# Splitting the remaining input projections into rounded pairs and reordering the first attention of a hybrid decoder block

## What is computed

```python
mod = silu(c) @ w_ada + b_ada            # 6 vectors of 1024: shift/scale/gate for mixer (a) and ffn (f)
h = rms_norm(x, g_attn) * (1 + sc_a) + sh_a
proj = h @ w_in                          # 1024 x 3072, cut into dq, dk, dv, sq, sk, sv (512 each)
# A: differential attention, 4 heads, two 64-wide q/k maps, 128-wide values, QK norm, ALiBi
a = softmax(q0 k0 + bias) - lam * softmax(q1 k1 + bias);  a_out = rms_norm(a @ dv) * 0.8
# B: stick-breaking attention, 8 heads of 64, strictly causal
a = exp(log_sigmoid(z) + suffix_sum(log_sigmoid(-z)));    b_out = rms_norm(a @ sv)
x = x + gt_a * (concat(a_out, b_out) @ w_out)
h = rms_norm(x, g_ffn) * (1 + sc_f) + sh_f
x = x + gt_f * hier_moe(h)               # top-1 of 4 groups, then top-2 of 8 SwiGLU experts of 256
```

## Time and profile before

| what | value |
|---|---|
| median of 3 runs | 682.06 us (679.41 to 684.06) |
| the profiled execution's own time | 682.16 us |
| its span | 680.0 us |
| PE busy | 561.3 us, 83% of the span, 2832 matmuls |
| DVE busy | 275.7 us, 41% |
| ACT busy | 170.2 us, 25% |
| chain that ended last | PE 67%, DMA 14%, SPq 7%, DVE 7%, ACT 3% |

### The profile page before, as it was taken

The page is one execution under the profiler, slowest core; times in us unless marked ns, Lnnn a source line. Parts: engine busy times, 40 slices in busy tenths (PEclk is TensorE's granted clock), DMA queues, the critical chain, the costliest instruction groups (busy, mean ns, idle before and its releaser), DMA issues.

```text
span 680.0 us, 7324 instructions
## 1 busy us (share of the span) xinstructions
PE 561.3 (83%) x2832; PEld 330.4 (49%) x2832; DVE 275.7 (41%) x474; ACT 170.2 (25%) x310; POOL 82.2 (12%) x98
## 2 busy tenths in 40 slices
PE   3379989999989899999999925988998898788740
PEld 2347768446455445665445613544554454344410
DVE  3866680553734455655012275222322232222005
ACT  7045541221222336786133210000000000000002
POOL 8331100000000000000021202111121112010000
PEclk9999999997998899999999955999999999889985
DMA  8984753537120007000751382899999999999719
GB/s 344 407 271 168 276 211 134 185 124 247 62 92 33 1 0 308 2 0 1 293 232 62 129 335 70 319 417 416 416 416 417 415 417 417 418 417 417 315 42 355
DMA packets 42384, 163.24 MB, mean 240 GB/s; under 512 B 7796, under 2 KB 7796, under 8 KB 34164
## 3 DMA queue, kind: packets, MB, share of 16 engines
q1 hardware_dynamic: 31972, 134.52, 49.6%
q0 software_dynamic: 9248, 26.23, 10.9%
q10 hardware_dynamic: 1136, 2.11, 0.8%
HBM read 158.64 MB, written 12.58 MB: 252 GB/s over the span
## 4 chain that ended last, share of the span: by engine, by line
PE 67%; DMA 14%; SPq 7%; DVE 7%; ACT 3%; issue 2%; POOLq 0%; DVEq 0%; ACTq 0%
PE banks L1582 11%; PE banks L1280 10%; PE banks L1474 8%; PE banks L1333 8%; PE banks L1601 6%; PE banks L1285 4%; DMA stage<-in_w_in_dram 4%; DMA stage<-in_w_dram 4%; DMA qkT<-in_w_dram 4%; PE banks L1426 3%; PE banks L1410 2%; PE banks L1570 2%; DMA stage<-pair_rows 2%; SPq L371 2%; PE banks L1355 1%
## 5 line engine op out<-in xcount | busy, mean ns | idle before, releaser
L1601 PE MATMUL banks<-stage,work 128*64 128x512 f32 x168 | 63.1, 638 | 10.0 <-ACT work L767 5.8
L1280 PE MATMUL banks<-hT,stage 128*128 128x512 f32 x144 | 66.4, 616 | 1.5 <-DMA stage<-in_w_in_dram 1.5
L1582 PE MATMUL banks<-qkT,work 128*64 128x256 f32 x272 | 63.6, 391 | 0.0
L765 ACT ACTIVATE work<-banks 128x256 f32<-128x256 f32 x16 | 6.1, 384 | 222.6 <-PE banks L1582 222.6
L1474 PE MATMUL banks<-stage,mixT 128*128 128x512 f32 x128 | 56.2, 594 | 0.0
L1185 DVE TENSOR_TENSOR work<-banks,gates 128x1024 f32<-128x1024 f32 x16 | 19.6, 1225 | 85.5 <-PE banks L1601 85.5
L1582 PE MATMUL banks<-hT,work 128*64 128x256 f32 x192 | 45.2, 394 | 2.6 <-DMA qkT<-in_w_dram 2.6
L799 DVE SCALAR_TENSOR_TENSOR mixT<-stage,small,mixT 128x1024 f32<-128x1024 f32 x35 | 44.9, 1282 | 3.5 <-DMA stage<-in_w_ada_dram 2.8
L1280 PEld LDWEIGHTS banks<-hT,stage 128*128 128x128 f32 x144 | 27.9, 199 | 34.0 <-issue 31.5
L1180 DVE TENSOR_TENSOR work<-work,banks 128x256 f32<-128x256 f32 x16 | 6.7, 421 | 88.3 <-ACT work L765 88.3
L534 POOL DMA_INDIRECT pair_rows<-work,tables x16 | 16.1, 1005 | 202.4 <-DVE work L1185 202.4
(11 more groups left out here) (263 smaller groups left out, 1089.4 us busy)
## 6 DMA issues: line engine op xcount, KB each, us to landing
stage<-in_w_dram SPq DMA_DIRECT2D x31, 1024.0 KB, 20.5
qkT<-in_w_dram SPq DMA_DIRECT2D x23, 1024.0 KB, 20.9
stage<-in_w_ada_dram POOLq DMA_DIRECT2D x16, 1024.0 KB, 5.6
stage<-in_w_in_dram SPq DMA_DIRECT2D x6, 2048.0 KB, 10.1
hT<-in_w_dram SPq DMA_DIRECT2D x12, 1024.0 KB, 18.2
val<-in_w_dram SPq DMA_DIRECT2D x10, 1024.0 KB, 18.4
mixT<-in_w_dram SPq DMA_DIRECT2D x10, 1024.0 KB, 18.6
alibi<-in_w_dram SPq DMA_DIRECT2D x5, 1024.0 KB, 23.6
```

The costliest lines, as they stand in the source:

```text
L1280: ins = mm(bank, w[:, k, ch * P:(ch + 1) * P], hT[:, k, :], start=(k == 0), stop=(k == KD - 1))
L1582: ins = mm(banks[half * C:(half + 1) * C, 2, up * F:(up + 1) * F], heT[:, r, k * P + half * C:k * P + (half + 1) * C], ws[2 * place + half ...
L1601: ins = mm(banks[half * C:(half + 1) * C, 4 + 2 * r + col, :], geT[:, fc * P + half * C:fc * P + (half + 1) * C], w2s[2 * place + half][:, ...
```

## The change

- **Jobs.** All 24 projection jobs run split now (`project`). Chunk 0 is rounded and subtracted by POOL; chunk 12 is rounded by ACT behind the last head evacuation, into a spare 128x1024 place (as chunk 16 later); chunks 13 to 23 are rounded in attention steps 0 to 8 (`split_at`), on ACT behind `exp_unit(s)` and on DVE behind `max_unit(s)` and the quarter.
- **Head order.** The two gate jobs stand ahead of the four v jobs.
- **Steps.** A step's jobs stand directly behind `scores(s)` on PE, ahead of `probT_make(s-1)`. Step 8 has no projection, step 15 has two halves; the column sum, the router product and the two late gate jobs move to steps 8, 12 and 14. The late adaLN quarters are summed in steps 0, 2, 4, 6, 8, 9, 10, 11.
- **Loads.** POOL's first adaLN quarter waits for the first piece of `w_in`; each gate bias row load stands behind its vector's quarters.
- **Memory.** `hT_hi` lies over x, `hT_lo` over `hT` itself; x is loaded again (2 MB) after the last v job, and POOL's additions wait for it. DVE does its four `hT_lo` subtractions after all eight `hT_hi` copies.

```diff
-    head = [("qk", n) for n in range(8)] + [("v", t, 0) for t in range(NT)] + [("gate", 0, 0), ("gate", 0, 1)]
+    head = [("qk", n) for n in range(8)] + [("gate", 0, 0), ("gate", 0, 1)] + [("v", t, 0) for t in range(NT)]
-        for _ in range(2 if s < 8 else 1):
+        for _ in range({8: 0, 15: 2}.get(s, 2 if s < 8 else 1)):
-    steps[7].append((("col", 3), None))
-    steps[9] += [(("gate", 1, 0), None), (("shift_router",), None)]
-    steps[11].append((("gate", 1, 1), None))
+    steps[8] += [(("col", 3), None), (("shift_router",), None)]
+    steps[12].append((("gate", 1, 0), None))
+    steps[14].append((("gate", 1, 1), None))
+ADA_STEPS = (0, 2, 4, 6, 8, 9, 10, 11)
...
+        hT_hi = rounded("hT_hi", [P, KD, T], "xr")
+        hT_lo = rounded("hT_lo", [P, KD, T], "hT")
+        w_hi_spare = rounded("w_hi_spare", [P, KD, P], "work", 3072)
...
+        def split_at(s):
+            return {0: (13,), 6: (19, 20), 7: (21, 22), 8: (23,)}.get(s, (s + 13,) if s < 6 else ())
+        def hi_before(n):
+            return {12: None, 16: 12, 20: 8}.get(n, n - 4 if n >= 4 else None)
```

SP, behind the loads of `w_in` and `w_out`:

```diff
             sp.wait_ge(job_done, job_no[("v", 3, 1)] + 1)
+            sp.dma_start(xr[:], x_rows).then_inc(x_again, 16)
```

POOL:

```diff
-            for n, v in enumerate((GATE_A, GATE_F)):
-                g.dma_start(gates[:, n, :], row(b_ada[:, v * D:(v + 1) * D])).then_inc(gate_bias_in, 16)
+            raw, hi, lo, arrived, value = split_chunk(0)
+            pool.wait_ge(arrived, value)
+            g.tensor_copy(hi, raw).then_inc(w0_hi, 1)
+            pool.wait_ge(w0_hi, 1)
+            g.tensor_tensor(lo, raw, hi.bitcast(F32), ALU.subtract).then_inc(w0_split, 1)
...
                     if n == 0:
                         pool.wait_ge(scale_used, KD // 2)
+                        pool.wait_ge(piece_in[0], 16)
...
+                for u, vec in enumerate((GATE_A, GATE_F)):
+                    if v == vec:
+                        g.dma_start(gates[:, u, :], row(b_ada[:, v * D:(v + 1) * D])).then_inc(gate_bias_in, 16)
+            pool.wait_ge(x_again, 16)
```

ACT:

```diff
-                if n >= 4:
-                    act.wait_ge(job_done, n - 3)
+                if hi_before(n) is not None:
+                    act.wait_ge(job_done, job_no[chunk_job(hi_before(n))] + 1)
+                if n == 12:
+                    act.wait_ge(norm_done, 8)
...
             for job in head_jobs:
                 job_evac(job)
+            w_round(12)
...
                 if s < NT * DH:
                     exp_unit(s)
+                for n in split_at(s):
+                    w_round(n)
```

DVE:

```diff
             for job in head_jobs:
                 job_evac(job)
+            w_rest(12)
...
-                if s < 8:
-                    ada_quarter(SCALE_F + s // 4, s % 4)
+                if s in ADA_STEPS:
+                    i = ADA_STEPS.index(s)
+                    ada_quarter(SCALE_F + i // 4, i % 4)
+                for n in split_at(s):
+                    w_rest(n)
```

PE:

```diff
+            def project(job, bank, ks):
...
+                if c == 0:
+                    pe.wait_ge(w0_split, 1)
+                    for k in ks:
+                        pe.wait_ge(hT_hi_ready, k + 1)
+                        mm(bank, w_hi[:, k, part], hT_hi[:, k, :], start=(k == 0), stop=False)
+                        mm(bank, lo[:, k, part], hT_hi[:, k, :], start=False, stop=False)
+                    pe.wait_ge(hT_lo_dve, KD // 2)
+                    pe.wait_ge(hT_lo_pool, KD // 2)
+                    for k in ks:
+                        ins = mm(bank, w_hi[:, k, part], hT_lo[:, k, :], start=False, stop=(k == KD - 1))
+                    return ins
+                pe.wait_ge(w_split, c)
+                hi = chunk_hi(c)
+                for k in ks:
+                    mm(bank, hi[:, k, :], hT_hi[:, k, :], start=(k == 0), stop=False)
+                    mm(bank, hi[:, k, :], hT_lo[:, k, :], start=False, stop=False)
+                    ins = mm(bank, lo[:, k, part], hT_hi[:, k, :], start=False, stop=(k == KD - 1))
...
                 if s < NT * DH:
                     scores(s)
+                for job, part in step_parts.get(s, ()):
+                    run(job, part)
                 if 1 <= s <= NT * DH:
                     probT_make(s - 1)
...
-                for job, part in step_parts.get(s, ()):
-                    run(job, part)
```

More of the change, by code:

```diff
@@ L1271, in run @@
                 kind = job[0]
-                if kind in ("qk", "sq", "sk"):
-                    n_in, ch = {"qk": (job[1] // 4, job[1] % 4), "sq": (3, job[1]), "sk": (4, job[1])}[kind]
-                    w, arrived, value = piece(n_in)
-                    pe.wait_ge(arrived, value)
-                    for k in ks:
-                        if n == 0:
-                            pe.wait_ge(hT_raw, k + 1)
-                        ins = mm(bank, w[:, k, ch * P:(ch + 1) * P], hT[:, k, :], start=(k == 0), stop=(k == KD - 1))
-                elif kind == "v":
-                    w, arrived, value = piece(2 if job[2] == 0 else 5)
-                    pe.wait_ge(arrived, value)
-                    for k in ks:
-                        ins = mm(bank, hT[:, k, job[1] * P:(job[1] + 1) * P], w[:, k, :], start=(k == 0), stop=(k == KD - 1))
+                if kind in ("qk", "sq", "sk", "v"):
+                    ins = project(job, bank, ks)
                 elif kind == "gate":
@@ L1310, in qk_norm @@
                 mm(banks[:, 2 + n % 2, :], halves, sqb[:, n % 2, :], start=True, stop=True).then_inc(norm_done, 1)
[L1312 to L1319 removed]
+            def project(job, bank, ks):
+                c = IN_JOBS.index(job)
+                lo = w_lo_parts[:, c // 4 % 2, :].rearrange("p (k n) -> p k n", k=KD)
+                if job[0] == "v":
+                    pe.wait_ge(w_split, c // 4 * 4 + 3)
+                    part = slice(job[1] * P, (job[1] + 1) * P)
+                    for k in ks:
+                        mm(bank, hT_hi[:, k, part], w_hi[:, k, :], start=(k == 0), stop=False)
+                        mm(bank, hT_hi[:, k, part], lo[:, k, :], start=False, stop=False)
+                        ins = mm(bank, hT_lo[:, k, part], w_hi[:, k, :], start=False, stop=(k == KD - 1))
+                    return ins
+                part = slice((c % 4) * P, (c % 4 + 1) * P)
+                if c == 0:
[4 more added lines that the diff above has]
+                        mm(bank, lo[:, k, part], hT_hi[:, k, :], start=False, stop=False)
@@ L1320, in run_split @@
                     pe.wait_ge(hT_lo_dve, KD // 2)
                     pe.wait_ge(hT_lo_pool, KD // 2)
-                lo = w_lo_parts[:, (2 if n >= 8 else n // 4) % 2, :].rearrange("p (k n) -> p k n", k=KD)
-                for k in range(KD):
-                    if job[0] == "qk":
-                        part = slice((n % 4) * P, (n % 4 + 1) * P)
-                        products = [(w_hi[:, k, part], hT_hi[:, k, :]), (w_hi[:, k, part], hT_lo(k)),
-                                    (lo[:, k, part], hT_hi[:, k, :])]
-                    else:
-                        part = slice(job[1] * P, (job[1] + 1) * P)
-                        products = [(hT_hi[:, k, part], w_hi[:, k, :]), (hT_hi[:, k, part], lo[:, k, :]),
-                                    (hT_lo(k)[:, part], w_hi[:, k, :])]
-                    for m, (still, moving) in enumerate(products):
-                        ins = mm(bank, still, moving, start=(k + m == 0), stop=(k == KD - 1 and m == 2))
@@ L1336, in _ @@
+                return ins
             for i, job in enumerate(head_jobs):
-                if i == 0 or job[0] == "gate":
-                    run(job)
-                else:
-                    run_split(job)
+                run(job)
                 if 1 <= i <= 8:
```

46 lines of the change are left out of this document (21 added, 25 removed).

## The result

The changed kernel takes 702.04 us, median of four (701.27 to 704.18), the kernel before 683.04 beside it (679.41 to 684.06): a ratio of 1.029, 95% interval 1.0245 to 1.0341. The profiled execution took 702.8 us with a span of 700.9, against 682.16 and 680.0. So the direction held and the size did not: +9.4 us forecast, 19 to 21 us measured, and 702 lies over the range.

A forecast was written before the change was run, and what follows sets the result against it. It took PE as the bound through the projections and first attention. From 682.16 us, terms of -3.5, +2.3, +11.1, -11.1 and -0.6 gave -1.8, and clock falls +11.2: 691.6 us, range 679 to 699.

The forecast's parts named there:

- Steps 0 to 7: From scores(0) to unit 6's transposes: each job waits for rounding behind the transposes, 77.6 us against 66.5, +11.1.
- the stretches behind: From unit 6's to unit 11's transposes: DVE is the bound, 33.4 us against 44.5, -11.1.
- PE stays the bound: Rival: ACT rounds chunks under the running projection, the 26.7 us of waits nearly vanish, 665 us; chance 0.06.
- The clock: Nine idle times on PE's path, three in four followed by a clock fall of 1.6 us: +11.2, bounds 0 and 20.
- the ninth: The last listed PE idle time, 2.9 us at step 15, priced like the others: three in four, 1.6 us a fall.
- What follows unit 15: Everything behind 256.7, untouched by the change: a shift there is carried to the end one to one.
- the stretch from unit 11 to unit 15: Steps 12 to 15: four halves save 2.8 us, a gate job adds 0.9, idle time 2.9; 22.0 for 22.6, -0.6.
- Gate jobs ahead of v: First v job waits for a gate job's bank, PE idles 4.7 us; v jobs end at 125.4 against 123.1, +2.3.
- Head: Start to qk job 1: first piece lands 7 to 8 us earlier, job 1 starts at 48.3, before 51.8: -3.5.
- The clock holds: Rival: the idle times are there but the clock stays at 2.4 GHz, 680.4 us, no change; chance 0.27.
- Heavier: Rival: POOL at 2.18 in the head (+3), every gap falling, some for two spells (+5): 699 to 700; chance 0.10.
- The split does nothing: Rival: a rounded trio costs 6.87 us like a float32 job, +11 on the forecast, 703 us; chance 0.02.

The follow-up runs named there:

- rounding first: The changed kernel with ACT rounding a step's chunks ahead of probT_evac(s-1) and exp_unit(s), no longer behind them: 671.53 us, ratio 0.986.
- the same, only where the wait is long: The changed kernel with 11 useless products on PE ahead of the waits for chunks 14, 15, 17, 18 and 19 alone: 694.67 us, ratio 1.020.
- all repairs together: The changed kernel with ACT rounding ahead, gate jobs behind v, chunk 12 rounded earlier, step 15's job behind unit 14's transposes: 666.04 us, ratio 0.975.

## Why the prediction was right or wrong

**Steps 0 to 7: right, with its mechanism.** The six waits of steps 2 to 7 were 3.9, 4.4, 5.2, 4.4, 3.9 and 4.4 us from the transposes to the job, for 4.1, 4.5, 5.0, 4.5, 4.1, 4.5. The idle times are 2.79, 2.75, 2.70, 2.51, 1.90 and 2.75, for "about 3.0 in the mean". The 87.8 us are 3.05 to the first sq job, 54.3 in the eight jobs, 0.6 for `scores(1)`, 3.6 for the column sum and 26.2 in the six waits; with the jobs at 5.46 that is 77.2, for a forecast of 77.6. The same for the stretches behind: -11.8 for -11.1, and the 2.44 us idle time ahead of unit 15, which the forecast had as 2.9. The rival *PE stays the bound* was priced at 665; the two kernels that take the order away ran 671.5 and 672.2, so roundings under the running job do what it said, and only the order of the changed kernel kept it from happening.

**The clock: right in kind, mis-sized, and this is the main failure.** The step was: seven of nine idle times, 1.6 us each, +11.2. In the steps the eight jobs took 7.2, 5.6, 7.1, 5.6, 7.9, 7.0, 5.6 and 8.4 us for 5.46: five slow ones at 1.5 to 2.9 us, 10.6 over all eight, where the seven idle times of the forecast in these steps come to 8.7 of the 11.2. That it is so near is in part luck, since the slow job of step 4 has its fall from the column sum ahead of it; the forecast had read the falls of the kernel before from idle times alone and had passed over the one at 159.1. The v jobs took another 1.6 (1.2 in the forecast). What broke it is the ninth, 1.2 us in the sum and 7.9 measured. The clock in single microseconds of the changed kernel:

```profile
271.00:272.00 1.00, 0.00 (x0) 0.00 (x0) 0.89 (x4) 0.88 (x2) 0.00 (x0) 1.00 0.95 385
272.00:273.00 1.00, 0.37 (x2) 0.38 (x3) 0.57 (x1) 0.00 (x0) 0.00 (x0) 0.55 1.00 401
273.00:274.00 1.00, 1.00 (x7) 1.00 (x6) 0.00 (x0) 0.22 (x1) 0.00 (x0) 0.50 0.99 410
...
291.00:292.00 1.00, 1.00 (x5) 1.00 (x5) 0.00 (x0) 0.16 (x1) 0.00 (x0) 0.50 0.00 0
292.00:293.00 1.00, 1.00 (x5) 0.82 (x5) 0.00 (x0) 0.75 (x2) 0.00 (x0) 0.71 0.00 0
```

The clock fell at about 272.1, in the idle time, and stood at 0.50, 1.2 GHz, until 292.6, with PE busy in every microsecond from 273: 20 us. What stands there up to 287.6 is narrow or thin work (64-row scores of the stick-breaking part, 128x128 transposes and `pv`), then products of 128x128 to 128x512. In the steps, where a job of 128x512 products follows the gap, the speed was back some 3 to 6 us into the job (149.07 to 152.5, 187.26 to 190.2, 208.08 to 214.1). The forecast priced a fall in one place by falls in another that were followed by dense products. That the thin products keep the clock low is a reading of these rows; no run put dense work behind that gap, and where the gap made no fall (*rounding first*) the same thin products ran at 1.00.

**What follows unit 15: wrong.** The step "I carry a shift at 256.7 to the end one to one" failed. The shift at 256.7 was +15.9, it grew to +23.9 behind the fall, and 3.0 came back later. Why is open. The part behind head 3's last transposes took from 400.0 to 404.9 us over the fourteen profiled kernels, and 404.8 in *the same, only where the wait is long*, whose instructions there are those of the changed kernel (401.7), so 3.0 us are within what this part varies by itself.

**The rest of the difference.** Of the 11.5 us between +9.4 and +20.9, the ninth idle time is 6.7, the head 5.0, the other falls 2.2, the stretch from unit 11 to unit 15 1.5 (cause not looked for), the part behind head 3 -3.0 and the remaining terms -0.9.

**Gate jobs ahead of v: right in kind, too low.** Start of the first v job 4.5 us idle (4.7 forecast), +2.3 in the sum and 1.6 for the clock; the stretch gave +4.1, so this term held. But undone it gives back 8.7: in the old place the gate jobs cover a part of the wait for chunk 12 too, and the forecast took that wait (2.56 us measured at the first sq job) as there in any case. It stands in the forecast's sum under steps 0 to 7.

**Head: wrong, -3.5 forecast, +1.5 measured.** The landing was right (about 35 us). Two terms failed. DVE's four subtractions for `hT_lo` ended at 49.8, not 46, because the six casts ahead of them took 0.88 us in the mean (single ones up to 1.52), not the 0.41 to 0.43 of the casts in the kernel before; the first two, with no subtraction on POOL beside them, took 0.43. And the eight products with `hT_lo`, alone behind an idle time of 2.95 us, took 3.45 us and not 1.8, at 1.2 GHz. The forecast had weighed the first, for POOL's subtractions only, and chose the lighter reading. These did stay light (1.27, 1.40, 1.41 and 1.65 us); it was DVE that waited. The trace of the kernel before shows this too, in DVE's subtractions for `hT_lo`: 0.69 us for the one ahead of POOL's, 1.63 to 1.64 for the three beside them, the first of these at 42.24 with POOL's begun at 41.96:

```profile
42.24 1.63 DVE L853 TENSOR_TENSOR hT_lo<-hT,hT_hi 128x512 fp32r<-128x512 f32 x1
```

The Trainium skill (SBUF — State Buffer, "SBUF: two separate sides") says that a GpSimd instruction and a VectorE instruction with two SBUF inputs, or in a two-port mode, each hold the shared pair of ports for the whole instruction, whichever starts first, and the other waits. The 8-column operation, begun behind POOL's and ended 0.02 us after it, agrees with it. The casts have one input, so they would fall under its other case, the two-port mode; which mode they ran in, no row shows.

**The rivals.** *The clock holds* fell: 0.84 in the long stretch. *Heavier* (699 to 700) was the nearest, but with the wrong content: POOL at its longest in every subtraction didn't happen (1.43 us in the mean), and two of the nine idle times had no fall; the 20 us at half speed behind unit 15 came in their place. *The split does nothing* fell: 5.6 us in the steps where the clock held.

## What to carry to other kernels

When a job is moved ahead on one engine, follow the circle through the others: whatever the next job needs must not stand, on any engine, behind something that waits for this one. Don't price an idle time of TensorE by one number: before dense 128x512 products gaps of 1.9 to 2.8 us cost nothing or 1.5 to 2.9 us here, before thin products the same gap of 2.44 us cost 6.7 to 8.0 in six profiles and 1.1 in two, and ten useless products in the gap took most of it back. Look too for falls with no gap, as behind the column sums. A move that saves engine time under a wait is worth nothing until the wait is cut; with it cut in either of two ways, the same split jobs gave 1.4 and 1.6% (2.4 to 2.5% with the other repairs) instead of costing 2.9%.

## What was not expected of the hardware

- TensorE busy at 1.00 in every microsecond from 273 and granted 0.50 of its clock for 20 us; and the same products behind the same idle time of 2.44 us at a clock of 1.00 in two other kernels, for some 9 us.
- A clock that fell in a column sum of 16 products of 128x1 with no idle time in the 27 us ahead of it (*all repairs together*, about 153.4).
- A VectorE operation on 8 columns that took 1.94 us beside a GpSimd subtraction and 0.17 without, and casts of 128x512 that took 0.41 to 0.43 us in the kernel before and up to 1.52 beside GpSimd's subtractions.
- In the kernel before, with only the order of the jobs changed, the same fall behind unit 15 stands in the profiled run (686.68 us, mean clock 0.933). An execution of the same kernel at 677.93 had a mean clock of 0.946, so the fall may have been short or missing in it, as in the profiles of two kernels above; only the first of the two was profiled, and the difference stays open.
